# Where one 16-byte tile stands in the order of the SBUF allocations

## The chip, the cores and the metric

The kernel runs on one core of one Trainium2 chip. The metric is the device time of one execution in microseconds (us); smaller is better. The kernel before was timed in three runs.

## The reference

Two model blocks follow each other on one sequence of 256 tokens of width 1024, all in fp32. The first has four layers, each an attention (differential, latent, dilated, differential) and a SwiGLU network of width 2816. The second has two layers of a mixer with three branches (pooling, convolution, attention over picked keys) and a gated network with a short convolution. What matters here is that nearly all the work is matrix products with weights read once from HBM:

```python
for i in range(DEPTH):
    h = rms_norm(x, attn_norm[i])
    x = x + mix(h)                      # A, B, C, A
    x = x + swiglu(rms_norm(x, ffn_norm[i]), f_w_gu[i], f_w_out[i])
x = rms_norm(x, final_norm)
...
# lambda of the differential attention: a number per layer
lam = exp(sum(lam_q1 * lam_k1)) - exp(sum(lam_q2 * lam_k2)) + lambda_init
```

## The kernel before

The activations stay in SBUF with features on the partitions: a tile such as `hT` or `h_hi` is 128 partitions by 8 feature blocks by 256 tokens. Weights stream from HBM in units of 128 by 2048 numbers (1 MB, in two transfers of 512 KB) into three slots `weights0` to `weights2`. ScalarE rounds each unit to `weights_hi` (L1330) and VectorE takes the rest as `weights_lo` (L1790), both in the type float32r. Activations are split the same way, into `h_hi` and `h_lo` in front of a projection, and `hid_hi`, `hid_lo` for the hidden layer.

Each product of a weight tile with an activation tile is three matmuls: high by high, high by low, low by high (`product`, L445). In nearly all of them the weights are the stationary operand, loaded into the array, and `h` or `hid` is the moving one; in `token_major` it is the other way round: 128 tokens of `h` are stationary and 256 columns of weights move. In the profile's names the moving operand stands first: `bank<-h_hi,weights_hi` has `h_hi` moving.

The other tiles that the change touches: `sq` (squares for the norms, and exponentials), `pres` and `rots` (projections out of PSUM and their rotated copies), `tab` and `rotm` (rotation tables and matrix), `ident` and `ones`, `pcol` (gains, biases and taps as columns), `brow`, and small ones for statistics. `lams` is 128 partitions by 4 numbers, 16 bytes on each partition. VectorE writes it once (L1841), ScalarE reads it once (L1731) for the lambdas.

**Where tiles start.** The program asks for the tiles one after the other. The allocator puts each behind the one before it and rounds its start up to a multiple of 32 bytes within the partition. The first, `weights0`, starts at byte 16,512, a multiple of 64. The nine weight tiles, `xT` and `hT` are 8,192 bytes each, so all of them start at multiples of 64 and `lams` starts at byte 106,624. It takes 16 bytes, and rounding makes it 32: `h_hi` starts at 106,656, which is 32 bytes past a multiple of 64. The tiles behind it, up to `brow`, have sizes that are multiples of 64, and so all start 32 bytes past a multiple of 64. From `eps` on the tiles are a few bytes each, and their starts alternate.

Behind the small tiles, at byte 155,168, begins an area that stages share: `Q`, `K` and `V`, or `o_hi` and `o_lo`, or `hid_hi` and `hid_lo`, or the second block's `G`, `Y`, `attn_hi`, `attn_lo`, `Z` and others. All of these start 32 bytes past a multiple of 64.

Of the kernel before, what the change touches and what calls it, by code (L numbers as in the profile page):

```python
# [32 lines left out]
P = 128  # L33
# [88 lines left out]
def build(nc, t, stages=99):  # L122

    with ExitStack() as ctx:
        def sb(name, shape, dt=F32, where=None):
            return (where or ctx).enter_context(nc.sbuf_tensor(name, shape, dt))
# [7 lines left out]
        w_lo = [sb(f"weights_lo{s}", [P, UNIT], F32R) for s in range(SLOTS)]  # L134
        xT = sb("xT", [P, KT, T])
        hT = sb("hT", [P, KT, T])
        lams = sb("lams", [P, 4])
        h_hi = sb("h_hi", [P, KT, T], F32R)
        h_lo = sb("h_lo", [P, KT, T], F32R)
        sq = sb("sq", [P, KT, T])  # L140
# [12 lines left out]
        esum = [sb(f"esum{i}", [P, 2]) for i in range(4)]  # L153
        erec = [sb(f"erec{i}", [P, 2]) for i in range(4)]
        tiny = sb("tiny", [P, 1])
        lame = sb("lame", [P, 4])
        neglam = sb("neglam", [P, 2])
        subg = sb("subg", [P, 2])
# [2374 lines left out]
```

## Time and profile before

| | |
|---|---|
| three runs | 2493.54, 2494.59, 2482.75 us; median 2493.54 |
| profiled execution: its time | 2493.54 us |
| profiled execution: span, first to last instruction | 2491.7 us |
| TensorE matmul busy | 2355.3 us (95%) |
| TensorE weight load busy | 2239.6 us (90%) |
| VectorE, ScalarE, GpSimd busy | 1514.8, 1137.7, 345.6 us |
| mean granted TensorE clock | 0.958 |
| mean DMA rate | 145 GB/s |

A matmul's busy time in the profile is its modelled duration, and matmuls overlap. What one costs is read from the distance between the starts of neighbours.

### The profile page before, as it was taken

The numbers are of one execution on the slowest core, as the hardware profiler recorded it, in microseconds if no ns is written. First come the engines' busy times: TensorE is split into PE (matmuls) and PEld (weight loads), VectorE is DVE, ScalarE is ACT, GpSimd is POOL, SyncE is SP. The second block draws the span as 40 slices with busy tenths as digits, with TensorE's granted clock in tenths as the row PEclk, the third lists the DMA queues.
The fourth block names the chain that finished last, engine by engine and source line by source line (L and its number), as shares of the span: only waits on it lengthen the run. The fifth ranks groups of instructions, "written<-read, shape, count | busy, mean of one in ns | idle before, by whom it ended". The sixth has DMA issues, their size and how long they took to land.

```text
span 2491.7 us, 45946 instructions
## 1 busy us (share of the span) xinstructions
PE 2355.3 (95%) x18456; PEld 2239.6 (90%) x18456; DVE 1514.8 (61%) x1923; ACT 1137.7 (46%) x1477; POOL 345.6 (14%) x448
## 2 busy tenths in 40 slices
PE   8899999999999999999999999878999999888998
PEld 7789997699999999999978999878789988868998
DVE  5746546455456566554665654668667557766763
ACT  4544344544345444443455343434355453345552
POOL 0002100012000000120300220480002109100210
PEclk9999998999999999999998999988899999989999
DMA  6327543156544444565541665334256544424651
GB/s 217 126 68 200 188 141 114 43 159 191 188 151 130 145 136 143 146 188 185 178 136 54 187 190 170 111 102 169 72 145 189 186 128 129 151 85 123 193 190 68
DMA packets 431039, 362.13 MB, mean 145 GB/s; under 512 B 20524, under 2 KB 404144, under 8 KB 430904
## 3 DMA queue, kind: packets, MB, share of 16 engines
q1 hardware_dynamic: 429128, 358.79, 46.9%
q8 instruction: 99, 1.62, 0.3%
q0 software_dynamic: 1264, 0.71, 0.1%
q10 hardware_dynamic: 512, 0.72, 0.1%
q14 instruction: 36, 0.29, 0.0%
HBM read 359.12 MB, written 1.05 MB: 145 GB/s over the span
## 4 chain that ended last, share of the span: by engine, by line
PE 81%; DVE 8%; POOL 6%; ACT 3%; issue 1%; DMA 0%; SPq 0%; ACTq 0%; DVEq 0%; POOLq 0%
PE bank L445 69%; POOL hT L1292 4%; DVE weights_lo L1790 2%; POOL Z L1294 2%; PE bank L476 2%; PE bank L559 2%; PE bank L548 2%; PE bank L777 1%; PE bank L791 1%; ACT weights_hi L1330 1%; PE bank L483 1%; PE bank L683 1%; PE bank L919 1%; PE bank L951 1%; PE bank L932 1%
## 5 line engine op out<-in xcount | busy, mean ns | idle before, releaser
L445 PE MATMUL bank<-h_hi,weights_hi 128*128 128x256 f32 (+1 forms) x3856 | 1113.6, 289 | 50.8 <-DVE h_lo L2208 16.6
L1790 DVE TENSOR_TENSOR weights_lo<-weights,weights_hi 128x2048 fp32r<-128x2048 f32 x343 | 788.6, 2299 | 607.7 <-ACT weights_hi L1330 605.2
L445 PE MATMUL bank<-h_lo,weights_hi 128*128 128x256 f32 (+1 forms) x3856 | 1090.6, 283 | 0.0
L445 PE MATMUL bank<-h_hi,weights_lo 128*128 128x256 f32 (+1 forms) x3856 | 1089.5, 283 | 0.0
L1330 ACT CAST weights_hi<-weights 128x2048 fp32r<-128x2048 f32 x343 | 654.1, 1907 | 561.8 <-PE bank L445 552.7
L445 PEld LDWEIGHTS bank<-h_hi,weights_hi 128*128 128x128 f32 (+1 forms) x3856 | 739.0, 192 | 67.8 <-issue 57.5
L445 PEld LDWEIGHTS bank<-h_lo,weights_hi 128*128 128x128 f32 (+1 forms) x3856 | 739.4, 192 | 9.4 <-issue 9.3
L445 PEld LDWEIGHTS bank<-h_hi,weights_lo 128*128 128x128 f32 (+1 forms) x3856 | 738.4, 191 | 0.0
L445 PE MATMUL bank<-hid_lo,weights_hi 128*128 (+1 forms) x1056 | 296.7, 281 | 0.0
L445 PE MATMUL bank<-hid_hi,weights_hi 128*128 (+1 forms) x1056 | 296.7, 281 | 0.0
L445 PE MATMUL bank<-hid_hi,weights_lo 128*128 (+1 forms) x1056 | 296.6, 281 | 0.0
L1243 POOL CAST hid_hi<-hT 128x256 f32 (+1 forms) x132 | 52.4, 397 | 1605.9 <-DVE hT L2170 1174.1
L445 PEld LDWEIGHTS bank<-hid_hi,weights_lo 128*128 128x128 f32 x1056 | 199.5, 189 | 0.0
L445 PEld LDWEIGHTS bank<-hid_hi,weights_hi 128*128 128x128 f32 x1056 | 199.5, 189 | 0.0
L445 PEld LDWEIGHTS bank<-hid_lo,weights_hi 128*128 128x128 f32 x1056 | 199.5, 189 | 0.0
L1245 POOL TENSOR_TENSOR hid_lo<-hT,hid_hi 128x256 f32 (+1 forms) x132 | 114.4, 867 | 19.7 <-POOL hid_hi L1243 17.8
L445 PE MATMUL bank<-weights_hi,h_hi 128*128 128x256 f32 (+2 forms) x360 | 107.2, 298 | 0.0
L2161 DVE TENSOR_TENSOR pres<-bank,hT 128x512 f32<-128x512 f32 x88 | 60.8, 691 | 71.7 <-PE bank L445 71.5
L445 PE MATMUL bank<-weights_lo,h_hi 128*128 128x256 f32 (+2 forms) x360 | 101.9, 283 | 0.0
L445 PE MATMUL bank<-weights_hi,h_lo 128*128 128x256 f32 (+2 forms) x360 | 101.7, 283 | 0.0
L1292 POOL TENSOR_SCALAR hT<-Z,pcol 128x256 f32<-128x256 f32 x60 | 94.9, 1581 | 0.0
L1710 ACT ACTIVATE pres<-bank,pcol 128x256 f32<-128x256 f32 x88 | 44.8, 560 | 91.3 <-PE bank L445 91.3
(292 smaller groups left out, 2502.9 us busy)
## 6 DMA issues: line engine op xcount, KB each, us to landing
weights<-in_f_w_gu SPq DMA_DIRECT2D x176, 512.0 KB, 5.0
weights<-in_f_w_out SPq DMA_DIRECT2D x88, 512.0 KB, 4.1
weights<-in_w_up SPq DMA_DIRECT2D x88, 512.0 KB, 5.0
weights<-in_w_in SPq DMA_DIRECT2D x82, 512.0 KB, 4.5
weights<-in_c_w_qkv SPq DMA_DIRECT2D x72, 512.0 KB, 4.5
weights<-in_a_w_qkv SPq DMA_DIRECT2D x48, 512.0 KB, 4.6
weights<-in_w_down SPq DMA_DIRECT2D x44, 512.0 KB, 3.8
weights<-in_a_w_o SPq DMA_DIRECT2D x16, 512.0 KB, 3.9
```

The costliest lines, as they stand in the source:

```text
L445: mm = nc.tensor.matmul(out, x, y, start=(first and n == 0), stop=(last and n == 2), skip_group_check=True)
L476: mm = nc.tensor.matmul(banks[bank][:, col + tt:col + tt + 1], src[:, j, tt * P:(tt + 1) * P], ones[:, 0:1], start=(n == 0), stop=(n == le ...
L548: mm = nc.tensor.matmul(banks[bank][:, 0:T], ones[:], src[:, j, :], start=(j == 0), stop=(j == KT - 1))
L559: close(nc.tensor.matmul(banks[r.bank][lo:hi, 0:n], rotm[lo:hi, m, lo:hi], pre[x.pre][lo:hi, 0:n], start=True, stop=True), r)
L1243: gp.tensor_copy(hid_hi[:, at], hT[:, j, :]).then_inc(hid_step, 1)
L1245: gp.tensor_tensor(hid_lo[:, at], hT[:, j, :], hid_hi[:, at].bitcast(F32), ALU.subtract).then_inc(hidden_ready, 1)
L1292: gp.tensor_scalar(hT[:, 2 + j % 2, :], hh, wj, None, ALU.mult).then_inc(conv_step, 1)
L1294: gp.tensor_tensor(conv_y[:, 0, :], conv_y[:, 0, :], hT[:, 2 + j % 2, :], ALU.add).then_inc(conv_step, 1)
L1330: nc.scalar.copy(w_hi[slot][:], raw[slot][:]).then_inc(hi_ready, 1)
L1710: ins = fn(pre[j][:, m * T:(m + 1) * T], banks[x.bank][:, m * T:(m + 1) * T], ACT.Identity, scale=col(w + tile + n), bias=col(b + tile + n))
L1790: v_.tensor_tensor(w_lo[slot][:], raw[slot][:], w_hi[slot][:].bitcast(F32), ALU.subtract).then_inc(lo_ready, 1)
L2161: free(v_.tensor_tensor(pre[j].rearrange("p (m n) -> p m n", m=2), banks[x.bank][:].rearrange("p (m n) -> p m n", m=2), hT[:, 4, :].unsque ...
```

## The change

`lams` is asked for later: behind `tiny` and ahead of `lame`, not between `hT` and `h_hi`. No instruction is added, removed or put elsewhere.

```diff
         xT = sb("xT", [P, KT, T])
         hT = sb("hT", [P, KT, T])
-        lams = sb("lams", [P, 4])
         h_hi = sb("h_hi", [P, KT, T], F32R)
         h_lo = sb("h_lo", [P, KT, T], F32R)
...
         tiny = sb("tiny", [P, 1])
+        lams = sb("lams", [P, 4])
         lame = sb("lame", [P, 4])
```

## Rows read from the trace of the kernel before

**Rows 1.** The cores' view: span and mean granted TensorE clock.
```profile
core 0: 2491.7 us, clock 0.958
```
**Rows 2.** The page: busy time of the engines, and the chain by engine and line.
```profile
PE 2355.3 (95%) x18456; PEld 2239.6 (90%) x18456; DVE 1514.8 (61%) x1923; ACT 1137.7 (46%) x1477; POOL 345.6 (14%) x448
...
PE 81%; DVE 8%; POOL 6%; ACT 3%; issue 1%; DMA 0%; SPq 0%; ACTq 0%; DVEq 0%; POOLq 0%
```
**Rows 3.** Tile view of h_hi, whole span: durations ns min/median/max, first and last start us.
```profile
L445 PE MATMUL bank<-h_hi,weights_hi x3856: 277/280/684, 14.4 to 2407.6; 128*128 128x256 f32 x191, 128*96 128x256 f32 x2
...
L445 PE MATMUL bank<-weights_hi,h_hi x360: 273/281/682, 74.0 to 2089.4; 128*128 128x256 f32 x160, 128*128 128x136 f32 x16, 128*128 128x512 f32 x4
```
**Rows 4.** The chain in order of time, two stretches: start us, us, what.
```profile
42.31 5.60 PE bank L445 x48
...
755.24 5.68 PE bank L445 x48
```
**Rows 5.** Tile view of h_hi on TensorE over those two stretches.
```profile
L445 PE MATMUL bank<-h_hi,weights_hi x16: 277/280/681, 41.7 to 47.4; 128*128 128x256 f32 x16
...
L445 PE MATMUL bank<-weights_hi,h_hi x16: 277/281/681, 754.7 to 760.4; 128*128 128x256 f32 x16
```
**Rows 6.** Timeline, two hidden stages: first and last of 28, then of 29 matmuls.
```profile
299.83 0.28 PE L445 MATMUL bank<-hid_hi,weights_hi 128*128 128x256 f32 x1
...
303.03 0.28 PE L445 MATMUL bank<-hid_hi,weights_hi 128*128 128x256 f32 x1
...
1959.81 0.28 PE L445 MATMUL bank<-hid_hi,weights_hi 128*128 128x256 f32 x1
...
1963.17 0.28 PE L445 MATMUL bank<-hid_lo,weights_hi 128*128 128x256 f32 x1
```
**Rows 7.** Source view of L548, fp32 matmuls with `ones` stationary.
```profile
L548 PE MATMUL bank<-sq,ones x96: 379/379/454, 1550.3 to 2479.1; 128*128 128x256 f32 x96
...
L548 PE MATMUL bank<-xT,ones x80: 377/379/766, 1558.8 to 2473.9; 128*128 128x256 f32 x80
```
**Rows 8.** Timeline of TensorE: first and last of 21 matmuls with 136 columns.
```profile
2084.15 0.27 PE L445 MATMUL bank<-weights_hi,h_hi 128*128 128x136 f32 x1
...
2086.38 0.27 PE L445 MATMUL bank<-weights_hi,h_lo 128*128 128x136 f32 x1
```
**Rows 9.** Source views of single lines on ScalarE and VectorE.
```profile
L1628 ACT ACTIVATE xT<-hT,pcol x40: 492/494/508, 1578.1 to 2485.1; 128x256 f32<-128x256 f32 x40
L1628 ACT ACTIVATE h_hi<-hT,pcol x32: 492/508/516, 1572.9 to 2286.6; 128x256 fp32r<-128x256 f32 x32
...
L2204 DVE SCALAR_TENSOR_TENSOR hT<-xT,pcol,sq x40: 476/478/486, 1572.4 to 2484.6; 128x256 f32<-128x256 f32 x40
...
L2208 DVE SCALAR_TENSOR_TENSOR h_lo<-hT,pcol,h_hi x32: 474/477/484, 1573.6 to 2287.3; 128x256 fp32r<-128x256 f32 x32
...
L1956 DVE TENSOR_TENSOR rots<-bank,hT x40: 682/684/685, 40.5 to 1274.5; 128x512 f32<-128x512 f32 x40
...
L1956 DVE TENSOR_TENSOR rots<-bank,tab x21: 411/680/686, 398.4 to 2095.6; 128x512 f32<-128x512 f32 x10, 96x512 f32<-96x512 f32 x8, 128x256 f32<-128x256 f32 x2, 32x256 f32<-32x256 f32 x1
```
**Rows 10.** Source views of the two lines that use `lams`.
```profile
L1841 DVE TENSOR_REDUCE lams<-K x1: 420/420/420, 30.2 to 30.2; 128x4 f32<-128x256 f32 x1
...
L1731 ACT ACTIVATE lame<-lams x1: 205/205/205, 30.6 to 30.6; 128x4 f32<-128x4 f32 x1
```
**Rows 11.** DMA issues: KB each, median us to landing, where it is known.
```profile
tab<-in_c_tab SPq DMA_DIRECT2D x1, 768.0 KB
```
**Rows 12.** Timeline of TensorE near the start: first and last of 9 matmuls.
```profile
15.17 0.41 PE L445 MATMUL bank<-h_hi,weights_hi 128*128 128x256 f32 x1
...
16.88 0.41 PE L445 MATMUL bank<-h_hi,weights_lo 128*128 128x256 f32 x1
```

## The prediction

> **What bounds the kernel now.** I first looked at the cores' view for the span and the clock: 2491.7 us at a mean granted clock of 0.958 [rows 1]. Then the page: TensorE is busy for 95% of the span, and the chain of work that ended last runs over it for 81% [rows 2]. VectorE and ScalarE are busy for about half the span and carry 8% and 3% of the chain, GpSimd 6%. So time changes by what changes the pace of the matmuls, and only a little by what changes a VectorE or ScalarE instruction.
>
> The tile view of `h_hi` gives the counts [rows 3]. A product has three matmuls, so `h` is the moving operand of 3 x 3856 = 11,568 matmuls, and the stationary one of 3 x 360 = 1,080, against 18,456 in all. The reader should see how large the lever is: 1 ns on each of the 11,568 is 11.6 us, or 0.46% of the kernel. A matmul's pace is read from stretches of the chain that hold one unit of 48: 5.60 us with `h` moving and the weights stationary, which is 116.7 ns each, and 5.68 us with `h` stationary, 118.3 ns each [rows 4, 5].
>
> **What the change does.** It moves addresses. Taking out `lams` removes 32 bytes (16, rounded up), so the tiles from `h_hi` to `brow` move down by 32 bytes and start at multiples of 64, where they started 32 bytes past one. That is `h_hi`, `h_lo`, `sq`, `pres`, `rots`, `tab`, `rotm`, `ident`, `ones`, `pcol`, `brow`. The small statistics tiles up to `tiny` move by 32 as well; their starts alternated before and alternate after. `lams` then fills the 32 bytes behind `tiny`, so that `lame` and all behind it, the shared area with `hid`, `o`, `attn`, `Q`, `K`, `V`, `Z`, stay where they are. So do the weights, `xT` and `hT`. The instructions, their order and their waits are the same. So the question is only whether an engine works at another pace on a tile that starts at 0 past a multiple of 64 than on one at 32. The trace has both kinds of tile, so each engine can be asked.
>
> **TensorE, moving operand (11,568 matmuls).** The cleanest pair is L548, an fp32 matmul over 256 columns with `ones` stationary: it moves `sq` (at 32) and `xT` (at 0). The medians are 379 and 379 ns [rows 7]. In the float32r products the start of the operand doesn't order the pace either. With a moving operand at 0 (weights, 118.3 ns) a matmul isn't faster than with one at 32 (`h`, 116.7 ns) [rows 4]. And `hid`, with operands at 32 against 0 as in `h`'s case, goes at (303.03 - 299.83)/27 = 118.5 ns in one layer and (1963.17 - 1959.81)/28 = 120.0 ns in another [rows 6]. So there is a spread of 3.3 ns between stages in which moving and stationary operand start just as they do for `h`; something else sets it. I take 0 us.
>
> The bounds. No product in this trace has both operands at 0, as the 11,568 will have. From above: if the 1.6 ns between rows with `h` moving and `h` stationary were the price of a moving operand at 0, it would come to 11,568 x 1.6 = +18.5 us. From below: the nearest row in which something shorter than the moving operand sets the pace is the one with 136 columns, (2086.38 - 2084.15)/20 = 111.5 ns [rows 8]. If the aligned start freed a matmul down to that pace it would give 11,568 x 5.2 = -60 us. The pair of L548 is nearest to this case and stands at neither end.
>
> **TensorE, stationary operand (1,080 matmuls).** `h` moves to 0 here while the weights move through the array from 0. If the 1.6 ns are the price of a stationary operand at 32, the change gives 1,080 x 1.6 = 1.7 us back; if not, nothing. I take 0, with -2 to +2 for the range.
>
> **The fp32 matmuls** on `sq`, `pres`, `ident`, `ones`, `rotm` have the answer of rows 7: 0.
>
> **ScalarE.** The same line writes `xT` (at 0) in a median of 494 ns and `h_hi` (at 32) in 508 [rows 9]. Part of that may be the output type. If all 14 ns went, at most the 8 such writes of each of 12 norms could see it, 96 x 14 ns = 1.3 us, and less, since most of them run while TensorE is still at work. I take 0, with -1.3 as the end; as the longer row is that of the tile that moves, nothing here speaks for a loss.
>
> **VectorE.** L2204 writes `hT` (at 0) in 478 ns, L2208 writes `h_lo` with `h_hi` as an input (both at 32) in 477. L1956 reads `hT` (at 0) as second operand in 684 ns and `tab` (at 32) in 680 [rows 9]. The differences have both signs and are under 1%. I take 0. VectorE's cover is TensorE, which is busy over it; without the cover, 4 ns on each of its 1,923 instructions would be 7.7 us, and by its 8% of the chain it is 0.6 us either way.
>
> **GpSimd** uses moved tiles only for taps in `pcol`, columns 8 bytes apart that fall on every kind of address before and after: 0.
>
> **DMA.** Weights land in tiles that stay. Of the moved tiles, `tab` is the largest target, 768 KB once, at the start [rows 11]: nothing waits for it but the first rotation, and if it took 1% longer that would be under 0.1 us.
>
> **`lams`** itself is used once, 420 ns on VectorE and 205 ns on ScalarE at 30 us, while TensorE has a unit of products to do [rows 10]. It stands at a multiple of 64 before and after: 0.
>
> **The sum** is 0, with small terms of -3.6 to +2.6 us. Against the profiled execution, 2493.54 us (span 2491.7 and 1.8 around it), that is 2493.5. This execution is the median of the three runs shown; they go from 2482.75 to 2494.59, so I put the median of new runs slightly below, at 2492 us. Differences up to 0.5% (12.5 us) count as no change here.
>
> **Rivals.**
>
> *Two operands in step make the array wait: slower.* Place: the 11,568 matmuls with `h` moving. For the first time both operands start at the same place within 64 bytes, and the weight load of the next matmul runs beside the stream of this one. If that costs the 1.6 ns of rows 4, the time is 2492 + 18.5 = 2510.5 us, slower by 0.7%; it decides from 1.1 ns a matmul on (12.5/11,568). Against it: L548 has `sq` and `ones` both at 32 and `xT` at 0 against `ones` at 32, and both take 379 ns. It is fp32, whose matmul is longer, so a small conflict could hide in it. Chance 0.05.
>
> *An aligned moving operand is faster.* 1,024 bytes from a multiple of 64 touch 16 pieces of 64 bytes, from 32 past one they touch 17. With the pace of rows 8 the time is 2492 - 60 = 2432 us; from 1.1 ns on it is a gain that can be measured. Against it are rows 7, and weights as moving operand, at 0, at 118.3 ns. Chance 0.04. The Trainium skill ("TensorE: Matmul & The Clock Gate", Back-to-back issue gap) gives N/2.4 + 2.5 ns, 109.2 ns for 256 columns, for a lone matmul, and a pace set by both load and stream in a real series. The trace's 116.7 ns are 7.5 over the lone figure; if all of it were the price of the start at 32, the sum by that rule would be an estimated 2492 - 87 = 2405 us. `hid` and weights as moving operand, slower at either start, speak against it.
>
> *The clock falls otherwise.* At the lower of its two levels (1.2 GHz) a product's matmul takes (16.88 - 15.17)/8 = 213.8 ns [rows 12], at 2.4 GHz 116.7. A stretch of t at the lower level costs 0.45 t, so 12.5 us need 28 us more or less of it, about 0.006 in the mean clock of 0.958. The change touches no wait that would bring this about; but small shifts could. The runs of before are 11.8 us apart without any change. Chance 0.05, half to each side; 2479 or 2505 us.
>
> *The change doesn't do what it says.* If the tiles didn't move, the result would be that of the forecast, which doesn't hang on it.
>
> **How the numbers follow.** No effect on any engine: 0.86, at 2492 us, with 2482 to 2500 as its own range (runs shown, and the small terms). Slower by conflict 0.05, faster by alignment 0.04, clock 0.025 on each side. Faster by over 0.5%: 0.04 + 0.025, about 0.065; slower: 0.05 + 0.025 = 0.075; the rest, 0.86, within. The range for 8 in 10 takes in the forecast case and the clock's two ends, 2479 to 2506 us; the conflict's 2510 and the gain's 2432 stay out, with 0.09 together.
>
> **What the profile of the changed kernel would show.** Right, if a unit of 48 with `h` moving takes 5.60 us again and one with `h` stationary 5.68 (or 5.60, if the stationary start mattered), L548 on `sq` 379 ns, ScalarE's writes of `h_hi` 494 to 508 ns, and VectorE's medians are within 4 ns. Wrong, if the units of 48 with `h` moving take other than 5.60 while `hid`, whose tiles don't move, keeps its pace: that is the conflict (5.68 and above) or the gain. If all paces stand and the time differs, look at the mean clock.

## The result: slower by 1.15%

The changed kernel takes 2518.62 us (median of four runs, 2517.49 to 2520.73), the kernel before 2491.39 us (four runs, 2482.75 to 2494.59). The ratio is 1.0115, with a 95% interval of 1.0089 to 1.0143. The forecast was no change, 2479 to 2506 us. The instructions are the same ones in the same order on every engine.

The profile after, first the cores' view, then the page's busy times and the chain by engine:

```profile
core 0: 2518.7 us, clock 0.957
```
```profile
PE 2389.1 (95%) x18456; PEld 2274.0 (90%) x18456; DVE 1517.0 (60%) x1923; ACT 1136.7 (45%) x1477; POOL 343.5 (14%) x448
...
PE 83%; DVE 6%; POOL 6%; ACT 3%; issue 1%; DMA 0%; ACTq 0%; DVEq 0%; POOLq 0%
```

Against [rows 1, 2] the span is 27.0 us longer. The clock (0.958 before), ScalarE, VectorE and GpSimd are as they were; only TensorE is busy for longer, by 2389.1 - 2355.3 = 33.8 us. The chain in order of time shows where. These are one unit with `h` moving, one stage of an up projection with its down projection (958 matmuls on `h` and 482 on `hid`), and one unit with `h` stationary:

```profile
41.84 5.75 PE bank L445 x48
...
188.32 171.53 PE bank L445 x1440
...
764.68 5.74 PE bank L445 x48
```

A unit with `h` moving went from 5.60 to 5.75 us, one with `h` stationary from 5.68 to 5.74 [rows 4], that is from 116.7 to 119.8 and from 118.3 to 119.6 ns a matmul. The stage of 1440 took 168.98 us before. Within such a stage, where nothing interrupts the stream, the distance between neighbouring starts with `h` moving went from 116.7 to 120.0 ns. What I had used as a witness for equal paces hasn't moved, and neither have the other engines:

```profile
L548 PE MATMUL bank<-sq,ones x96: 379/379/455, 1570.2 to 2506.1; 128*128 128x256 f32 x96
...
L1628 ACT ACTIVATE h_hi<-hT,pcol x32: 491/508/512, 1592.9 to 2310.8; 128x256 fp32r<-128x256 f32 x32
...
L2208 DVE SCALAR_TENSOR_TENSOR h_lo<-hT,pcol,h_hi x32: 475/479/482, 1593.6 to 2311.5; 128x256 fp32r<-128x256 f32 x32
```

But `hid`, whose tiles stand where they stood, changed too. The timeline of TensorE in its first hidden stage, first and last of 28:

```profile
309.93 0.28 PE L445 MATMUL bank<-hid_hi,weights_lo 128*128 128x256 f32 x1
...
313.10 0.28 PE L445 MATMUL bank<-hid_hi,weights_lo 128*128 128x256 f32 x1
```

That is (313.10 - 309.93)/27 = 117.4 ns, where [rows 6] have 118.5 and 120.0. The stage of 1440 says the same: 3.3 ns more on 958 matmuls are 3.2 us, 1.3 ns less on 482 are 0.6, and it grew by 2.55.

**The 27 us add up.** 11,568 matmuls with `h` moving are 241 units: 241 x 0.15 = +36.2 us (over all of them the mean distance between neighbouring starts went from 116.8 to 119.9 ns). 1,080 with `h` stationary: 22.5 x 0.06 = +1.4. 3,168 on `hid`, 1.1 to 1.3 ns less each: about -4. Together +33.6, against 33.8 more busy time. TensorE's idle time fell from 136.4 to 129.6 us. Most of that is one row of its waits, before:

```profile
PE bank L445 <- DVE weights_lo L1790: 14.4, 3, 6.9
```

and after (us in total, times, longest):

```profile
PE bank L445 <- DVE weights_lo L1790: 7.7, 2, 4.7
```

VectorE had more time to split the next weights while the slower products ran, and 6.7 us came back there.

### The profile page after: what moved, and what is told of

It reads as the page before. It is cut to its first block, busy times and chain, and to the rows that moved or that the text cites. A ratio compares the mean times of both kernels' runs of the same rounds, so it can differ in the third digit from the quotient of the medians.

```text
span 2518.7 us, 45946 instructions
## 1 busy us (share of the span) xinstructions
PE 2389.1 (95%) x18456; PEld 2274.0 (90%) x18456; DVE 1517.0 (60%) x1923; ACT 1136.7 (45%) x1477; POOL 343.5 (14%) x448
## 4 chain that ended last, share of the span: by engine, by line
PE 83%; DVE 6%; POOL 6%; ACT 3%; issue 1%; DMA 0%; ACTq 0%; DVEq 0%; POOLq 0%
PE bank L445 72%; POOL hT L1292 3%; POOL Z L1294 2%; PE bank L476 2%; DVE weights_lo L1790 2%; PE bank L559 2%; PE bank L548 2%; PE bank L777 1%; PE bank L791 1%; ACT weights_hi L1330 1%; PE bank L483 1%; PE bank L683 1%; PE bank L919 1%; PE bank L951 1%; PE bank L932 1%
## 5 line engine op out<-in xcount | busy, mean ns | idle before, releaser
L445 PE MATMUL bank<-h_hi,weights_hi 128*128 128x256 f32 (+1 forms) x3856 | 1127.6, 292 | 43.8 <-DVE h_lo L2208 16.6
L445 PE MATMUL bank<-h_lo,weights_hi 128*128 128x256 f32 (+1 forms) x3856 | 1105.2, 287 | 0.0
L445 PE MATMUL bank<-h_hi,weights_lo 128*128 128x256 f32 (+1 forms) x3856 | 1105.0, 287 | 0.0
L445 PEld LDWEIGHTS bank<-h_hi,weights_hi 128*128 128x128 f32 (+1 forms) x3856 | 753.6, 195 | 60.6 <-issue 51.2
L445 PEld LDWEIGHTS bank<-h_lo,weights_hi 128*128 128x128 f32 (+1 forms) x3856 | 753.4, 195 | 9.4 <-issue 9.3
L445 PEld LDWEIGHTS bank<-h_hi,weights_lo 128*128 128x128 f32 (+1 forms) x3856 | 752.6, 195 | 0.0
L1292 POOL TENSOR_SCALAR hT<-Z,pcol 128x256 f32<-128x256 f32 x60 | 88.6, 1477 | 0.0
```

The source lines that it names most:

```text
L445: mm = nc.tensor.matmul(out, x, y, start=(first and n == 0), stop=(last and n == 2), skip_group_check=True)
L1292: gp.tensor_scalar(hT[:, 2 + j % 2, :], hh, wj, None, ALU.mult).then_inc(conv_step, 1)
```

## The experiments

What separates the theories is what about the addresses counts. *Theory 1*: the moving and the stationary operand slow each other when they start at the same place within 64 bytes. *Theory 2*: a moving operand at a multiple of 64 is slow by itself. *Theory 3*: the pace is a state of an execution that has nothing to do with addresses. I call **distance** the start of the moving operand minus that of the stationary one, modulo 256 bytes. It is 32 for `h` in the kernel before and 0 after; 224 and 0 where `h` is stationary; 160 for `hid`, `o`, `attn`, `pool` and `conv` in both.

**The kernel before once more.** No edit. 

> The kernel before, unchanged, profiled again. If the pace of the products is set by where the operands stand (theory 1 and theory 2), each stage keeps its pace: 116.7 ns a matmul with h moving, 118.3 with h stationary, and the hidden stages again 118.7, 117.3, 118.7, 118.7, 120.0, 118.7 ns in this order; time 2491 us. If the pace is a state that an execution falls into (theory 3), stages come out at other paces, up to 120 ns with h moving, and the time may be anywhere between 2480 and 2520.

2494.47 us (ten runs, 2488.8 to 2499.38), ratio 1.0013 (0.9997 to 1.0029). One unit, then two of the stages of 1440:

```profile
41.97 5.60 PE bank L445 x48
...
1031.32 168.98 PE bank L445 x1440
...
1376.23 169.62 PE bank L445 x1440
...
2283.11 188.80 PE bank L445 x1584
```

The same last stage, of 1584 matmuls, in the first profile:

```profile
2283.13 187.65 PE bank L445 x1584
```

Units with `h` moving are at 5.60 again. But the stage at 1376 takes 169.62 us, where the first profile had 168.98, by its matmuls on `hid`; and in the last stage it is `h` that goes at 117.8 ns, where it went at 116.7. A few stages changed pace, one way or the other, with the same addresses. So an address doesn't fix a pace entirely, and theory 3 is weakened by this run and not refuted; what refutes it are the kernels below that have `h` at distance 0, where every long stage on `h` goes at 120.0 ns.

**Only `h_hi` and `h_lo` moved.** `lams` behind `h_lo`:

```diff
-        lams = sb("lams", [P, 4])
         h_hi = sb("h_hi", [P, KT, T], F32R)
         h_lo = sb("h_lo", [P, KT, T], F32R)
+        lams = sb("lams", [P, 4])
```

> lams stands behind h_lo: h_hi and h_lo start at multiples of 64, all other tiles stand as in the kernel before. Theory 1 (the weights and the moving operand at the same place within 64 bytes slow each other) and theory 2 (a moving operand at a multiple of 64 is slow): a matmul with h moving takes 119.9 ns, the time is 2518 us or a few us more (the hidden stages keep their old paces, 118.7 ns on average). Rival, that sq, pres, tables or the small tiles cost the time: 2491 us and 116.7 ns.

2518.21 us, ratio 1.0110 (1.0083 to 1.0137):

```profile
42.83 5.75 PE bank L445 x48
...
189.36 171.53 PE bank L445 x1440
```

The whole loss is there. `sq`, `pres`, tables and the small tiles have no part in it.

**Only `h_hi` moved.** `lams` between `h_hi` and `h_lo`.

> lams stands between h_hi and h_lo: only h_hi moves to a multiple of 64. Two of three matmuls of a product have h_hi moving, one h_lo. If each matmul pays by its own operand (theories 1 and 2): two thirds of the loss, about 2509 us, and 118.8 ns a matmul on average, with steps that repeat in threes. If one aligned operand is enough to break the step: 2518 us. If all must be: 2491 us.

2498.5 us (ten runs, 2491.87 to 2507.18), ratio 1.0028 (1.0012 to 1.0043), less than the two thirds I had expected. The units in the chain are of two kinds:

```profile
42.12 5.63 PE bank L445 x48
48.62 5.75 PE bank L445 x48
```

With two of three matmuls of a product at distance 0 the same code runs at 5.63 or at 5.75 us a unit, and executions are up to 15 us apart. So I stopped thinking of a price per matmul: there are steady paces, and a unit is in one or the other.

**The products alone.** A kernel that leaves the model out. It loads x, splits it, and runs lines of 96 matmuls in the order of `product`, no other engine at work, each line with its own starts. This is L64, with the moving operand 8 numbers, 32 bytes, on:

```python
for r in range(2):
    for n, (a, c, h, w, z) in enumerate(STEPS): ins = mm(banks[1][:, 256 * z:256 * z + 256], w[:, a + c + 0:a + c + 0 + 128], h[:, a + 8:a + 8 + 256], ...)
```

> The model is left out; the kernel only runs products of three float32r matmuls over 128x128 and 256 columns, 96 in a line, with the start of the stationary and of the moving operand set line by line, and no other engine at work. Theory 1: about 117 ns a matmul (11.2 us a line) where the two starts differ within 64 bytes and about 120 ns (11.5 us a line) where they are equal (0 and 0, 0 and 64, 32 and 32, 32 and 96). Theory 2: 120 ns wherever the moving operand starts at a multiple of 64, whatever the stationary one does, so 0 and 0, 32 and 0 slow, 32 and 32 fast. Theory 3 (no address effect): all lines equal.

The chain in order of time. In the lines shown the stationary operand stands at 0 and the moving one at 32, 0 and 64 bytes (L64, L66, L76); then the stationary one at 32 and the moving one at 32, 64 and 96 (L84, L88, L90):

```profile
21.29 11.20 PE bank L64 x96
32.49 11.52 PE bank L66 x96
...
89.49 11.31 PE bank L76 x96
...
134.92 11.50 PE bank L84 x96
...
157.82 11.20 PE bank L88 x96
169.03 10.88 PE bank L90 x96
```

Both paces of the model are here without the model: 11.20/96 = 116.7 ns at 32, 11.52/96 = 120.0 at 0. Theory 2 falls: with the moving operand at 64 and the stationary one at 32 (L88) it is 116.7, and with both at 32 (L84) 119.8. Theory 1 holds for distance 0, but its "within 64 bytes" falls: distance 64 (L76, L90) isn't 120 but 117.8 or 113.3. It is the distance that counts, over a longer period. L76 and L90 have the same distance and two paces.

**More distances.** The same kernel, stationary at 0, the moving operand at 0 to 256 in steps of 32 and at 512, then back in the opposite order, then pairs. 

> The model is left out; products alone, 96 matmuls a line, no other engine at work. Theory 1 in its new form (only the distance between the two operands' starts counts, moving minus stationary, and it repeats after 128 bytes): with the stationary one at 0, distances 0 to 512 in steps of 32 give 11.5, 11.2, 10.9 or 11.3, 11.4, and again from 128 on; the same distance gives the same time wherever the pair stands. Rival (each line's pace also depends on the pace it starts from): the same distances in the opposite order, or 64 after another distance than before, give another time, by up to 0.4 us a line.

These are 0, 32, 64, then 128, 192 and 256 of the way out; then, on the way back, 192, 64 and 32:

```profile
20.98 11.51 PE bank L64 x96
32.50 11.31 PE bank L66 x96
43.81 11.31 PE bank L68 x96
...
66.63 11.39 PE bank L72 x96
...
89.28 10.91 PE bank L76 x96
...
111.55 11.51 PE bank L80 x96
...
168.99 11.31 PE bank L90 x96
...
214.60 10.89 PE bank L98 x96
225.49 11.21 PE bank L100 x96
```

128 isn't like 0 (118.6 against 119.9 ns), 256 is: the pattern repeats after 256 bytes, as far as these distances show, not after 128 as I had expected. And 32, 64 and 192 give another time on the way back: 117.8 or 116.8 at 32, 117.8 or 113.4 at 64, 113.6 or 117.8 at 192.

**`h` at 64, the shared area at 192.** A second 16-byte tile beside `lams`, so that `h` and the shared area stand 32 bytes further on. Both are 64 bytes from a multiple of 256, on one side or the other.

```diff
         lams = sb("lams", [P, 4])
+        sb("apart", [P, 4])
```

> A second 16-byte tile stands beside lams: against the kernel before, h_hi to tiny and the shared area stand 32 bytes further on, so all moving operands start 64 bytes past a multiple of 128, at a distance of 64 (or minus 64) from the weights. Distance theory with the paces of the products alone (113.3 ns at 64): h saves 3.4 ns on 11,568 matmuls, hid 5.4 on 3,168, the rest 4 on some 500: 2491 - 58 = 2433 us. If any start at a multiple of 64 is slow (old theories 1 and 2): 119.9 ns, 2520 us or more. If the pace at 64 hangs on the pace it starts from (117.8 ns, as in one of three lines): 2500 us.

2486.41 us, ratio 0.9988 (0.9972 to 1.0005). The gain forecast from 113.3 ns didn't come. With `h` moving every long stage goes at the slow one of two paces, 117.8 ns, which is the third case; but `hid` goes at 113.4 in two of its six stages, and the time is the old one and not 2500 us. Two of the stages of 1440, `hid` slow in the first and fast in the second:

```profile
182.59 169.62 PE bank L446 x1440
...
1024.41 167.49 PE bank L446 x1440
```

**Weights and `h` both at 32.** The kernel after with 32 bytes in front of all tiles:

```diff
+        sb("apart", [P, 4])
         raw = [sb(f"weights{s}", [P, UNIT]) for s in range(SLOTS)]
```

> The kernel after with 32 bytes in front of all tiles: weights, xT, hT and h all start 32 bytes past a multiple of 64, at distance 0 from each other; the shared area keeps its distance to the weights. Distance theory: as slow as the kernel after, 2518 us, 119.9 ns with h moving. Theory 2 (a moving operand at a multiple of 64 is slow): h is at 32 again, so 2491 us and 116.7 ns.

2519.11 us, ratio 1.0117 (1.0087 to 1.0148), with `h` back at 32 past a multiple of 64:

```profile
41.88 5.75 PE bank L446 x48
...
187.32 171.53 PE bank L446 x1440
```

In the model too it is the distance, not the place.

**Only the shared area moved.** The kernel before with a tile behind `tiny`; `hid` and the others come from distance 160 to 192, `h` stays at 32.

```diff
         tiny = sb("tiny", [P, 1])
+        sb("apart", [P, 4])
```

> The kernel before with a 16-byte tile behind tiny: only lame and what follows, with the shared area, stands 32 bytes further on. h keeps distance 32, and hid, attn, o, pool and conv come to a distance of minus 64 from the weights. Distance theory: h stays at 116.7 ns, hid goes from 118.7 to 113.3 ns: 3,168 x 5.4 ns = 17 us, and some 2 us for the others, 2472 us. Rival, that the pace of hid is inherited from the h stage in front of it (118.7 after 116.7, 117.3 after 119.9): 2491 us.

2470.05 us, ratio 0.9926 (0.9906 to 0.9946), as forecast:

```profile
42.60 5.60 PE bank L446 x48
...
183.40 166.43 PE bank L446 x1440
```

`hid` goes at 113.4 ns in five of its six stages and at 117.8 in the last.

**Different starts.** Theory 4: the distance allows one or two steady paces, and how a stretch starts picks one. Theory 5: the pace before it picks. A kernel of products alone again; each line of 48 begins after TensorE has waited for a VectorE copy of another length:

```python
ins.then_inc(turn, 1)
pe.wait_ge(go, 2)
for n, (a, c, h, w, z) in enumerate(STEPS): ins = mm(...)
```

> The model is left out; lines of 48 products' matmuls, each started after TensorE has waited for a VectorE copy of another length, so that each starts at another moment; seven lines for each distance 64, 32, 192, 160, 0 and 224, two for each of nine distances in between, then fp32 lines. If the distance allows one or two steady paces and the start picks one (theory 4): distances 0 and 224 give one pace (119.9 and 118.3 ns), 64 and 192 some lines at 113.4 and some at 117.8, 32 at 116.7 or 117.8, 160 at 117.3 or 118.7. If the pace before the line picks (theory 5): all lines of a distance alike. The fp32 lines: one pace at all distances, about 220 ns, so that they show nothing of the float32r products; if they differ with the distance too, the fp32 pair was a fair test and the prediction misread it.

Distance 64 has lines L73 to L91, 32 L94 to L112, 192 L115 to L133, 160 L136 to L154, 0 L157 to L175, 224 L178 to L196, seven each. Two of 64, two of 192, one of 0 and one of 224, then two of the twelve fp32 lines (distances 0 and 32; 24 matmuls each, in two records a matmul):

```profile
29.64 5.72 PE bank L73 x48
35.67 5.94 PE bank L76 x48
...
116.92 5.74 PE bank L115 x48
122.96 5.93 PE bank L118 x48
...
203.91 6.02 PE bank L157 x48
...
248.53 5.96 PE bank L178 x48
...
405.92 10.64 PE bank L253 x48
416.90 10.64 PE bank L256 x48
```

All lines of distance 0 are at 6.02 or 6.03 us and all of 224 at 5.95 or 5.96: one pace. At 64 two are at 5.72 and five at 5.93 or 5.94; at 192 five at 5.72 or 5.74 and two at 5.93; at 32 five at 5.88 or 5.89 and two at 5.93; at 160 four at 5.91 or 5.92 and three at 5.98. Lines of a distance follow each other and still differ, so theory 5 alone falls and theory 4 is left. The nine distances in between, 8 to 88 bytes, take 5.88 to 6.08 us: steps smaller than 32 bytes count too, and 0 isn't the slowest distance of all. All twelve fp32 lines take 10.64 us, at six distances.

The traces of the whole model say two more things, read from the distances between neighbouring starts. In all ten of them no uninterrupted stretch of 72 or more products' matmuls on `h` or `hid` changes its pace once it is under way. And where `hid` follows `h` without a break, the pace of `h` goes with the one that `hid` gets, at the same distance of 160. After `h` at 116.7 or 117.8 ns, in the two traces of the kernel before, the twelve hidden stages go at 118.7 (eight), 120.0 (three) and 117.3 (one). After `h` at 120.0 ns they go at 117.3 in 19 stages of 19: six each in the kernel after, in the one with `h_hi` and `h_lo` moved and in the one with weights and `h` at 32, and one with only `h_hi` moved, whose other five go at 118.7 after `h` at 117.0. The first and last of 28 matmuls of that one:

```profile
1961.07 0.28 PE L445 MATMUL bank<-hid_lo,weights_hi 128*128 128x256 f32 x1
...
1964.24 0.28 PE L445 MATMUL bank<-hid_lo,weights_hi 128*128 128x256 f32 x1
```

That is 117.4 ns. So the pace ahead isn't without effect; by itself it doesn't decide.

**All at 192, and only `h` at 192.**

```diff
         lams = sb("lams", [P, 4])
+        sb("apart_h", [P, 40])
...
         tiny = sb("tiny", [P, 1])
+        sb("apart_area", [P, 32])
```

The second kernel has 24 in place of 32, so that the shared area keeps distance 160.

> Tiles set apart so that h_hi, h_lo and the tiles behind them, and the shared area too, start 192 bytes (within 256) past the weights. Theory 4 (the distance allows a fast and a slow steady pace, 113.4 and 117.8 ns, and the start of a stage picks one): if five of seven stages are fast, as among the starts tried, h takes 114.7 ns on average, 2.0 less than before on 11,568 matmuls, and hid 114.1 in place of 118.7: 2491 - 23 - 17 = 2451 us, with single executions 20 us apart. If h never falls into the fast pace (as nearly never at 64): 117.8 ns, 2491 + 12 - 17 = 2486 us.

> Only h_hi to tiny stand 192 bytes past the weights; the shared area keeps its distance of 160. Theory 4: h as in the kernel with all tiles at 192 (114.7 ns on average, or 117.8 if it stays slow), hid at 117.3 or 118.7: 2468 us, or 2503 us. If the gain of hid at 192 came from the pace of h in front of it, hid would be at 113.4 here as well and the time 2451 us.

All at 192: 2462.14 us (six runs, 2452.41 to 2473.43), ratio 0.9890 (0.9862 to 0.9919), the fastest version here. Two stages of its chain:

```profile
181.84 163.24 PE bank L447 x1440
...
1349.41 169.62 PE bank L447 x1440
```

Only `h` at 192: 2474.74 us, ratio 0.9951 (0.9930 to 0.9973):

```profile
182.55 165.15 PE bank L447 x1440
...
1018.59 169.40 PE bank L447 x1440
```

The same code takes 163.24 or 169.62 us, according to the pace its stages fell into. The forecast of 2451 us for the first took five stages of seven at the fast pace. It came out 11 us above that: in the profiled execution `h` averages 115.0 ns and not 114.7, `hid` 114.8 and not 114.1, which is 6 us of it, and the rest stays open. The second came out 7 us above its 2468, with `h` at 115.3 ns. That `hid` gains only if its own distance changes is confirmed: in the second kernel 165.15 less 163.24, 1.9 us a stage, is missing. With all at 192, `hid` goes in all six of its stages at the pace of the `h` in front of it, 113.3 or 117.8 ns. With only `h` at 192 it goes at 117.3 five times and at 118.7 once.

## Why the prediction was wrong

- **What bounds the kernel** was right. TensorE's pace sets the time, 1 ns on the 11,568 matmuls is 11.6 us, and 3.1 ns more on average made +36.2 us of it.
- **The step that failed** is the one on TensorE's moving operand, "I take 0 us". It asked each operand for its own place modulo 64. The pace of a float32r product hangs on the distance between its two operands, and repeats after 256 bytes as far as that was measured. The change took this from 32 to 0, the slowest of the distances that the model's tiles had, with one pace only. I had written that no product of the trace had both operands at 0, and priced the conflict at +18.5 us; it is +36.2. The place and the sign of that rival were right, its price half of what was measured and its chance of 0.05 far too low.
- **Why the chance was low.** First, the pair of L548 in [rows 7]. It is a fair pair of distances, 0 for `sq` (both it and `ones` at 32) and 224 for `xT`, but it is fp32, and twelve fp32 lines at six distances all take 10.64 us. It could not have shown anything of the float32r products; the prediction named this doubt and then let the pair decide. Second, the spread in [rows 6], 118.5 and 120.0 ns for `hid`, was taken as proof that something other than addresses sets the pace. It was the sign of the effect: several steady paces for one distance. The lines of products alone show 117.3 and 118.7 at 160; 120.0 at 160 appeared only in the model.
- **`hid`** was to keep its pace, also by the rival's own sign. It went from 118.7 to 117.3 ns on average, about -4 us that no term had.
- **The stationary operand** of 1,080 matmuls was put at -2 to +2 us and measured +1.4, by the same mechanism (distance 224 to 0), not by its own place.
- **The fp32 matmuls, ScalarE, VectorE** at 0: right. ScalarE's 508 ns for `h_hi` stayed 508 at its new place, so the 14 ns of [rows 9] don't come from the start.
- **GpSimd, DMA, `lams`**: no sign of a change; with `h_hi` and `h_lo` alone moved the whole loss is there.
- **The sum** had no term for what a slower TensorE gives back. The waits for `weights_lo` shrank by 6.7 us. The low end of its small terms adds up to -3.9 us (-2, -1.3 and -0.6), not -3.6, which changes nothing else.
- **The estimate by the Trainium skill's figure** took the 7.5 ns above the lone figure for the price of the start at 32, which would have given -87 us. A gain exists, but at another distance and smaller: the lowest steady pace seen is 113.4 ns. The Trainium skill ("TensorE: Matmul & The Clock Gate", Back-to-back issue gap) says that in a stream of load and matmul the pace is set by both; the runs agree so far as the pace depends on where the two stand to each other, 113.4 to 120.0 ns with the same instructions. The same page (Step-by-step: what each phase is for) says that loading the next weights takes no read bandwidth from the running matmul. No run here measures bandwidth, but the two operands aren't independent in time: with no other engine at work a matmul takes 119.9 ns at distance 0 and as little as 113.4 at 64. For the time of a matmul the measurement decides.

**Shown and not shown.** Shown: the loss lies in the float32r products that touch `h`, it follows the distance in the model and alone, and several distances (32, 64, 160, 192) allow two or more steady paces, one of which a stretch gets where it starts and then keeps. Not shown: what inside the chip makes it so. That the reads of the two operands get in each other's way is a guess that no run here tests. Nor is it shown what about a start picks the pace, beyond the pace ahead having a part in it. The executions of one kernel are 10 to 27 us apart, and 2 to 3 us at distance 0. Paces that are picked anew have a part in that, but so has the clock: of 19 executions of the kernel before, the shortest, 2483.36 us, had a mean granted clock of 0.961 and the longest, 2499.15 us, one of 0.955. With all at 192 the clocks are 0.958 and 0.956 for 2452.41 and 2473.43 us; by the prediction's own price, 12.5 us for 0.006, they account for about 4 us (an estimate) of 21.

## What to carry to other kernels

In a stream of float32r products of 256 columns, each with its own load of weights, the bytes between the starts of the two tiles are worth a sweep by themselves: here 2462 to 2519 us with the same instructions. Other widths were not swept, and of the other types only fp32 was, which showed nothing. A small tile allocated between large ones decides this silently, so the distance is best set on purpose, with a gap. Moving the small tile out of the way isn't enough: the tiles here have sizes that are multiples of 256 bytes, and side by side they stand at distance 0, which is the kernel after. And ask the trace about pairs of operands in the same data type, not about one operand; a spread between stages of equal code is a finding to be explained before it is used as a reason.

## What the runs showed that I had not expected

- Steady paces of a float32r matmul with 256 columns, from the products alone: 120 ns at distance 0 and 96, 118.6 at 128, 118.3 at 224, 117.3 or 118.7 at 160, 116.7 or 117.8 at 32, 113.4 or 117.8 at 64 and 192.
- A pace holds over more than a hundred microseconds: stages of 1440 matmuls come out at 171.53 us four times of four in the kernel after, with `h` at distance 0, and with all at 192 at 163.24 three times and 169.62 once (within 0.01).
- Part of what an engine loses can come back in its waits for others: 33.8 us more of busy time were 27.0 us of span.
